# Four tiles of x turned in front of the first product instead of five, the fifth behind its first half

## What is computed

```python
for layer in range(2):
    h = rmsnorm(x, norm_w[layer])
    if layer % 2 == 0:
        proj = h @ ev_w_in[i]           # 1024 -> 2304 columns
        u, g_a, q, k, v, g_b = split_cols(proj, [512, 512, 512, 128, 128, 512])
        a_out = s5_mixer(u, ...) * silu(g_a)        # diagonal complex state space
        b_out = swa_mixer(q, k, v, ...) * silu(g_b)  # sliding-window attention
        mix = concatenate([a_out, b_out]) @ ev_w_out[i]
    else:
        ...                              # gated linear attention, the same form
    x = x + mix
return rmsnorm(x, final_norm)
```

## Time and profile before

| | us |
|---|---|
| median of 3 executions | 1708.22 (1706.62 to 1710.53) |
| the profiled execution, device time | 1708.07 |
| its span, first to last instruction | 1706.3 |
| TensorE busy | 1646.2 (96%) |
| DVE busy | 822.5 (48%) |
| ACT busy | 631.0 (37%) |
| POOL busy | 277.8 (16%) |
| mean granted clock of TensorE | 0.992 |

### The profile page before, as it was taken

How to read it: one execution, slowest core, us unless ns; L and a number is a source line. 1 busy time by engine, 2 the same in 40 slices (tenths; PEclk the granted TensorE clock), 3 DMA queues, 4 the chain that set the end, 5 groups by cost and what they waited for, 6 DMA issues and landing times.

```text
span 1706.3 us, 22568 instructions
## 1 busy us (share of the span) xinstructions
PE 1646.2 (96%) x7898; PEld 1334.1 (78%) x7898; DVE 822.5 (48%) x1655; ACT 631.0 (37%) x1584; POOL 277.8 (16%) x500
## 2 busy tenths in 40 slices
PE   6999899999999799999999999999999999999997
PEld 4777687777777578888778888888888888878886
DVE  6744444666676374553452333434333443354443
ACT  6522333666666473233361222222222332131221
POOL 3883000000000341110000122222222221000000
PEclk9999999999999899999999999999999999999999
DMA  5466444554444847222243332333323322266663
GB/s 214 144 189 185 137 130 139 154 151 144 144 133 125 255 133 259 74 100 90 74 148 109 102 126 97 118 109 115 114 99 109 124 95 86 98 232 190 191 191 109
DMA packets 222216, 236.18 MB, mean 138 GB/s; under 512 B 53112, under 2 KB 169496, under 8 KB 222104
## 3 DMA queue, kind: packets, MB, share of 16 engines
q1 hardware_dynamic: 221528, 233.59, 43.6%
q10 hardware_dynamic: 576, 1.15, 0.2%
HBM read 140.12 MB, written 94.57 MB: 138 GB/s over the span
## 4 chain that ended last, share of the span: by engine, by line
PE 61%; DVE 1%; ACT 1%; DMA 1%; issue 0%; SPq 0%; POOLq 0%; POOL 0%; DVEq 0%; ACTq 0%
PE odd_bank L2143 29%; PE odd_bank L2298 10%; PE odd_bank L2189 10%; PE odd_bank L2168 2%; PE odd_bank L2248 2%; PE odd_bank L2245 2%; PE odd_bank L2246 2%; PE odd_bank L2227 1%; PE odd_bank L2152 1%; PE odd_bank L2203 1%; DMA scr_heads<-odd_ga_min 1%; PE odd_bank L2229 0%; PE odd_bank L2256 0%; PE odd_bank L2230 0%; PE odd_bank L2255 0%
## 5 line engine op out<-in xcount | busy, mean ns | idle before, releaser
L2143 PE MATMUL odd_bank<-ht_hi,odd_w_hi 128*128 128x512 f32 x768 | 318.4, 415 | 0.0
L2143 PE MATMUL odd_bank<-ht_lo,odd_w_hi 128*128 128x512 f32 x768 | 300.6, 391 | 0.0
L2143 PE MATMUL odd_bank<-ht_hi,odd_w_lo 128*128 128x512 f32 x768 | 298.9, 389 | 0.0
L1214 PE MATMUL ev_acc<-ht_hi,ev_w_hi 128*128 128x512 f32 x576 | 240.0, 417 | 2.4 <-DVE ht_lo L926 2.4
L1214 PE MATMUL ev_acc<-ht_hi,ev_w_lo 128*128 128x512 f32 x576 | 226.8, 394 | 0.0
L1214 PE MATMUL ev_acc<-ht_lo,ev_w_hi 128*128 128x512 f32 x576 | 226.6, 393 | 0.0
L1919 DVE COPY odd_stage<-odd_bank 128x512 f32<-128x512 f32 x96 | 66.4, 692 | 224.7 <-PE odd_bank L2143 224.7
L2143 PEld LDWEIGHTS odd_bank<-ht_lo,odd_w_hi 128*128 128x128 f32 x768 | 144.1, 188 | 31.8
L2143 PEld LDWEIGHTS odd_bank<-ht_hi,odd_w_hi 128*128 128x128 f32 x768 | 144.4, 188 | 30.0 <-issue 3.0
L2143 PEld LDWEIGHTS odd_bank<-ht_hi,odd_w_lo 128*128 128x128 f32 x768 | 144.7, 188 | 27.7
L1214 PEld LDWEIGHTS ev_acc<-ht_hi,ev_w_hi 128*128 128x128 f32 x576 | 109.0, 189 | 30.8 <-issue 5.5
(11 more groups left out here) (284 smaller groups left out, 2880.8 us busy)
## 6 DMA issues: line engine op xcount, KB each, us to landing
odd_gl_in<-scr_heads SPq DMA_DIRECT2D x32, 640.0 KB, 4.3
scr_heads<-odd_stage SPq DMA_DIRECT2D x64, 256.0 KB, 2.2
odd_w_raw<-od_w_in SPq DMA_DIRECT2D x24, 512.0 KB, 4.0
ev_w_raw<-ev_w_in SPq DMA_DIRECT2D x17, 512.0 KB, 6.4
ev_s_cos_sin<-scr_s_cos_sin SPq DMA_DIRECT2D x32, 256.0 KB
odd_xo_sum<-x SPq DMA_DIRECT2D x16, 512.0 KB, 4.1
scr_x<-odd_xo_sum SPq DMA_DIRECT2D x16, 512.0 KB, 2.9
scr_gla_mix<-odd_gl_out SPq DMA_DIRECT2D x32, 256.0 KB, 2.1
```

The lines of the kernel that those rows point to most:

```text
L1214: mm = pe.matmul(acc[n % 3][:], w[j][:, k, :], h[:, k, t], start=(k == 0 and r == 0), stop=(k == KT - 1 and r == 2))
L2143: mm = pe.matmul(acc[n % 4][:], w[j][:, k, :], h[:, k, t], start=(k == 0 and q == 0), stop=(k == KT - 1 and q == 2))
```

## The change

TensorE turns the tiles 0 to 3 in front of its loop and no longer tile 4. Tile 4 is turned behind the first half of the first product, and tile 5 right behind it, where it stood before. From there on the order is the same. Nothing else is changed; the queues of the other engines keep their order, and every wait keeps its value.

```diff
                 pe.wait_ge(ident_in, 16)
-                for t in range(5):
+                for t in range(4):
                     turn_x(t)
                 for p in range(p_end):
                     n = p // 2
...
                             products(n, KT // 2).then_inc(acc_full, 1)
+                    if p == 0:
+                        turn_x(4)
                     if p + 5 < NT:
                         turn_x(p + 5)
```

## The result

The changed kernel takes 1714.43 us (median of 9 executions, 1710.67 to 1718.31) against 1708.22 us (9 executions, 1706.57 to 1710.53). The ratio is 1.0037, with a 95% interval of 1.0027 to 1.0046: slower by 0.37%, some 6 us. Both are clear of no change, and each median lies in the range of the prediction; the forecast was +4.5.

What follows compares the result with a forecast made beforehand. The prediction took TensorE's own stream (busy 1646.2 of 1706.3 us) to set the end. Terms 0, 0.81 and 3.74 gave +4.55, carried as +4.5: 1708.2 + 4.5 = 1712.7 us, range 1708.0 to 1716.0.

Steps and rivals of the forecast that it cites:

- The removed turning gains nothing: Before the first product: taking `turn_x(4)` away leaves its start at 26.55, since it waits for `lower(3)`; term 0.
- The chain: First stage: late `upper(4)` holds up `sines()`, `square(6)`, root and `normed(6)`, so `turn_x(6)` waits 3.7 us, until 40.0.
- The sum of +4.55: At `turn_x(6)`: 0.81 us for the turning in a busy TensorE plus 3.74 us of new wait.
- its larger term, the wait: Before `turn_x(6)`: TensorE's new wait for DVE's line 920, 3.74 us.
- Carried to the end: Behind the first stage: all queues move along with TensorE's delay, so +4.5 us reaches the end.
- given back: Rival: the wait of 5.42 us near 184 us shrinks as a store lands sooner; 1707.3 us, chance 0.17.
- The clock in the new wait: Rival at the wait before `turn_x(6)`: the clock falls too, some 1.65 us lost, partly hidden; chance 0.12.
- The rival's time, 1714.1: Whole kernel if the clock falls in the new wait too: +4.5 + 1.4 = 5.9 us; chance 0.12.
- the likeliest case: Whole kernel: the wait and its carry as laid out, 1712.7 us, own range 1710.7 to 1714.7; chance 0.64.
- The rise at the start: At the first product: the moment the clock rises could shift, 1.3 us either way, put in the range.
- The drains of the table loads: In ACT's `sines()`: each of two loads followed by a pause as long as itself, 7.1 us, 1715.3; chance 0.03.

Runs made afterwards that it cites:

- e5: The changed kernel itself measured once more, against the kernel before: 1713.18 us against 1708.94, ratio 1.0027.
- e8: The kernel before, with 23 matmuls whose sums nobody reads in TensorE's idle times between the first five turnings: 1704.25 us against 1708.94, ratio 0.9967.
- e10: The changed kernel with both idle stretches of TensorE filled with added matmuls, ahead of the first product and of `turn_x(6)`: 1708.38 us against 1709.94, ratio 0.9997.
- e1: The changed kernel with `sines()` moved from behind `upper(4)` to behind `square(5)`: 1710.03 us against 1708.94 for the kernel before, ratio 1.0005.
- e4: Control: the kernel before with `sines()` and `square(6)` put ahead of `upper(4)`: 1709.27 us against 1708.94, ratio 1.0001.
- e6: The kernel before with `lower(3)` put ahead of the DVE step of `set_up()` that stood in front of it: 1704.82 us against 1708.94, ratio 0.9979.
- e3: The changed kernel with 14 matmuls whose sums nobody reads put ahead of `turn_x(6)`: 1712.42 us against 1708.94 for the kernel before, ratio 1.0017.

## Why the prediction was right, and where not

- **The removed turning gains nothing.** The first product started at 26.61, predicted 26.55, and was released by line 926. Right.
- **The chain.** Every link of it kept its length. (POOL's round of turns took 1.22 us, not the predicted 2.28; it was over 1.31 us before the root's turn, so it was not on the path.) The table loads began at 32.70, predicted about 33.5; `turn_x(6)` ran at 39.17, predicted 40.0. The chain is some 0.84 us early, because the first half took 30.98 - 26.61 = 4.37 us, not 5.25: the clock rose earlier in that execution. The wait was 3.53 us, predicted 3.74, and `turn_x(6)` came 3.72 us later than in the earlier trace rows, in the profile of e5 4.32.
- **The sum of +4.55.** Shown by e8 and e10 (+4.36 at the same turning). That its larger term, the wait, comes from `sines()` and `square(6)` behind `upper(4)`, and not from the turning in the full stream, is shown by e1 (the wait falls to 0.42 us) with its control e4.
- **Carried to the end.** In the profile after the delay at the last turning is 76.57 - 71.18 = 5.39 us and 4.7 at the end; in that of e5 7.01 and 7.0. The wait near 184 us kept some 5.3 us in all three profiles, so the case "given back" did not come about there. But the delay was not carried through unchanged. At the matmuls of line 1251 it is 272.02 - 265.67 = 6.35 us, and behind them the clock falls in the profile after alone. At the border of the layers the granted clock averages 0.66 over 577 to 597 us in the profile before and 0.74 over 584 to 604 in the profile after, 1.6 us less lost. At the wait of 1.9 us in the second layer the delay is 635.16 - 628.99 = 6.17 us, and there the clock falls in the profile before alone. Such a fall costs some 1.7 us (0.43 x 4), so a difference between two single profiles holds the chance of where the clock fell, and that 4.7 is so near to 4.5 is in part luck. The medians are what carries the result.
- **The clock in the new wait: the step that failed.** I gave it 0.12, because the gap seemed nearer to the one of 2.80 us, behind which the clock had stayed up. That rested on one wait in one execution. In the eleven other profiles the clock fell behind the same wait, at 2.87 us in the profile after, and the profile before itself had a fall behind a wait of 1.91 us, at 628.99. In the new wait it fell in both profiled executions, once just behind the wait and once within it. The price was 1.58 us in one profile, as predicted (1.65), and 2.65 in the other, where the lower level lasted twice as long. The Trainium skill (TensorE: Matmul & The Clock Gate, HAM oscillation), cited with the prediction, says that bursts with waits between them fall back to the low clock; both profiles of the changed kernel agree with it, at a wait of 3.53 us each. The rival's time, 1714.1, is nearer to the first median (1714.43, 6.2 us above the kernel before) than the forecast of 1712.7. The second, 4.2 to 4.6 us above its own kernel before, is at the forecast's +4.5. So in the profiled executions the likeliest case was the wrong one of two on the same side, and the range held since it took in both. That the second measurement meets +4.5 does not show the sum to be whole: in its profile it is made up differently, with 2.65 us of the clock in it.
- **The rise at the start.** I put it at 1.3 us either way. It was wider: the first half took 4.37 us in one profile of the changed kernel and 5.26 in the other, some 3.4 in e6, and in e3 even `turn_x(4)` behind it was slow.
- **The drains of the table loads** (0.03): the second load ended at 35.67 and `square(6)` started at 35.69. No pause.

Left open: in how many executions the clock falls in the wait, and thus how the 4.6 and the 6.3 us of the two measurements divide.

## What to carry to other kernels

When a step is taken out of an engine's idle time, look at what stands behind its consumer in the other queues: here a copy that came 6.8 us later held up table loads and a square that had nothing to do with it, and the wait cost over four times the step itself. If such a step has to come later, move what stands behind its consumer ahead of it. And an idle stretch of TensorE that costs nothing in the order of work can still cost by the clock: the cheapest gain here was to let the first product start sooner and TensorE stand less. To judge whether the clock falls in a wait, look at the same wait in several profiles: one that shows no fall, as the wait of line 1251 here, can be the exception.

## What the runs showed of the hardware

- With an idle stretch of 3.53 us the granted clock fell in both profiles, to 0.50, for some 3.4 us in one and 6.8 us in the other. With 2.80 us it did not in the profile before; with 2.87 and 2.56 us at the same wait it did in the two profiles of the changed kernel (0.57 over the four us behind). With 1.9 us it fell at 628.99 in the profile before and not at 635.16 in the profile after. The length of the one wait before did not decide it. The fall can begin after the engine is at work again: in the profile after, the matmuls from 40.02 on are slow, the turnings at 39.17 and 39.66 (0.65 and 0.60 us) are not.
- From the start of the first product to the rise it took 1.3 us in e6, where no idle time stood before the product, and 3.1 us after 5.24 us of idle time in the profile after; in e3, after 5.28 us, it took some 6. With TensorE kept busy from 10 us on (e8) the turnings from 15.76 on were already fast.
- The clock column shows 1.00 at the start of every profile here, though the durations there are those of 1.2 GHz. Where no fall has been recorded yet, the durations are what to read.
